# Seven half-width products for a pair of tiles: z, ga, gdn out and mix, and the attention's query and output

## The chip, the cores and the metric

One core of a Trainium2 chip runs the kernel. The metric is the device time of one execution in microseconds; the median of three runs stands for the kernel. A profile shows one execution, with every instruction of every engine. All data are float32.

## What is computed

Three blocks, one behind the other, on one sequence of 512 tokens and a width of 1024. The change lies in the first block: a gated feed-forward layer (ffn1), layer norm (ln1), "parallel mixers", layer norm (ln2), cross attention to a memory of 256 tokens, layer norm (ln3), a second feed-forward layer (ffn2), layer norm (ln4). Cut to what matters:

```python
def parallel_mixers(h, ...):
    proj = h @ w_in                       # qkv, z, a, bt, glu, gates
    ...
    o = chunk_gated_delta_rule(...)
    o = rms_norm(o, gdn_norm_g) * jax.nn.silu(z)
    y_a = o @ w_gdn_out
    ...
    y = jax.nn.sigmoid(g_a) * y_a + jax.nn.sigmoid(g_c) * y_c
    return y @ w_mix_out

def memory_cross_attention(x, mem, w_xq, w_xkv, w_xo):
    q = x @ w_xq
    k, v = jnp.split(mem @ w_xkv, 2, axis=-1)
    o = softmax(q @ k.T / 16) @ v         # 4 heads of 256
    return o @ w_xo
```

Both results y enter `x = layer_norm(2 ** 0.25 * x + y)`. The products in question are z, g_a (called ga), y_a (gdn out), the last line of the mixers (mix), q (xq) and the last line of the attention (xo): each a matrix of 1024 x 1024 on 512 tokens.

## The kernel before, in words

**Data.** Activations lie transposed: a tile has 128 features on the partitions and 512 tokens along them, so a vector of width 1024 is eight tiles. `X` (tiles 0 to 7) is the running activation; `main` is one large SBUF buffer in which `mem(at, tiles)` names places. Weights stream through four slots `w0` to `w3`, one load of 1 MB for each pair of output tiles (eight input tiles x two output tiles), issued by SyncE in the order in which TensorE takes the slots (`sp_weights`, L446): a load waits until the slot's last user is done ("w used"). PSUM has eight banks, handed out round robin (`banks.take`); whoever takes a bank waits for the "out" of its last user. Some stages confine the turn to a subset (`banks.only(range(2, 8))` in ssd and hgrn, `range(1, 8)` in rwkv), each subset with a counter of its own.

**Order.** Each engine has its program written out in order: `pe_...`, `act_...`, `dve_...` functions run over the same steps. Nothing is reordered; an engine that waits holds up all that stands behind it. Steps are named, and `wait_ge(*at(step))` waits for a named one.

**A pair** (`pe_pair`, the matmul at L262): for two output tiles f, eight matmuls each (k = 0 to 7) of 512 columns, 16 in all. Input tile k is waited for just before its matmul. ScalarE or VectorE then reads each bank.

**A step of seven** (`pe_seven`, the matmul at L338), used so far in the feed-forward layers and in the second and third blocks: input tiles are taken in pairs, tokens in two halves of 256, so that a pair of output tiles is a 2 x 2 block product, and the scheme of Strassen and Winograd gives it with seven products in place of eight. A product is four matmuls of 256 columns (one for each pair of input tiles), a step 28. The operands that are sums are made by VectorE: `dve_seven_weights` (L387, L388, L390, L392: four operations of 512 columns per step) and `dve_halves` (L401, L404, L406: once per pair of input tiles, not per step). The results are put together from four banks: `act_seven` copies the first one (L377), `dve_seven_out` does four operations (L422, L425, L427, L430), the last behind the last product. TensorE's order is product 1, 2 (from the input itself), 4 (needs all halves), 6 (needs the weight sums), 5, 7, 3. The sums have two places that alternate (`sets`).

**The mixers' end** (`pe_mixers`, L898). Behind the delta rule ("gdn", L1118 to L1298) come the head sums (L574), then the z pairs, with two spreads of the reciprocal root (L597) behind each, then ga, gdn out and mix, four pairs each. ScalarE takes z through SiLU (L998) and ga through a sigmoid (L1001). VectorE scales `O1` by the spread (L1060), multiplies it by the gate (L1064, "gated"), multiplies gdn out by its gate (L1068), adds the convolution's part (L1070, "mixed"), and at mix does the residual (`dve_residual`, L720) and a running total for the mean (L481). SyncE issues the loads of z only behind gdn (`input_here("after gdn")`).

**ln2 and ln3** (`pe_ln`): the sum of the total (L461) gives the mean, VectorE centres (L542), ScalarE squares (L499), TensorE adds the squares (L470), then root, reciprocal (L514), scaling (L547) and ScalarE's scale and bias (L535). At ln2 two pairs of xk run between mean and squares, and two behind the squares; they have 256 columns (the memory's tokens).

**The attention** (`pe_xattn`, L1357): xk's last two pairs, xq's four pairs with ScalarE's copies to `QT` (L1404), scores (L1372), softmax, values (L307), probabilities transposed (L1382), the attention's output (L1394), copied to `O2` by ScalarE (L1423), and xo's four pairs with VectorE's residuals (L720).

The lines that say how an engine takes a bank and how the residual is made:

```python
            for f in range(m):
                b, before = into[f]
                if kg == 0 and before:
                    pe.wait_ge(*at("out", *before))
                for k in range(kk):
                    pe.wait_ge(*at(*g.ready, kg + k))
                    i = pe.mm(PS[b][:, 0:n], wv[:, k, f * 128:(f + 1) * 128], g.X(kg + k),
                              start=kg + k == 0, stop=kg + k == g.nk - 1)
```

Of the kernel before, what the change touches and what calls it, by code (L numbers as in the profile page):

```python
# [14 lines left out]
TOK = 512  # L15
NT = 4
D = 1024
ALPHA = 2.0 ** 0.25
# [169 lines left out]
def assemble(nc, ctx, io, out):  # L188
# [27 lines left out]
    def mem(at_, tiles, width=TOK):  # L216
        return View(main[:, at_:at_ + tiles * width].rearrange("p (a b) -> p a b", b=width))

# [497 lines left out]
    def dve_residual(v, name, ready, total):  # L716
        for f in range(8):
# [132 lines left out]
    G_z = Gemm("z", w_in, 3072, 8, 8, X, x1)  # L850
    G_ga = Gemm("ga", w_in, 6160, 8, 8, X, x1)
    G_gout = Gemm("gdn out", io["w_gdn_out"], 0, 8, 8, O1, ("gated",))
    G_mix = Gemm("mix", io["w_mix_out"], 0, 8, 8, YC, ("mixed",))
# [44 lines left out]
    def pe_mixers(pe):  # L898
# [31 lines left out]
        for j in range(0, 8, 2):  # L930
            run(pe_pair(pe, G_z, j))
            for i in (j, j + 1):
                pe_head_spread(pe, "o1", i)
        run(pe_gemm(pe, G_ga))
        run(pe_gemm(pe, G_gout))
        run(pe_gemm(pe, G_mix))
        pe.fence("mix")

    def act_mixers(a):
# [56 lines left out]
        for f in range(8):  # L996
            a.wait_ge(*at("mm", "z", f))
            a.act(Z1(f), bank("z", f), ACT.Silu).then_inc(a.inc(s, "out", "z", f), 1)  # L998
        for f in range(8):
            a.wait_ge(*at("mm", "ga", f))  # L1000
            a.act(GA(f), bank("ga", f), ACT.Sigmoid).then_inc(a.inc(s, "out", "ga", f), 1)  # L1001
        a.fence("mix")

    def dve_mixers(v):
# [50 lines left out]
        s = sem["dve", "gdn"]  # L1055
        dve_head_root(v, "o1", 32, 7, 1.0 / 128, 1e-6)
        dve_head_rstd(v, "o1", 32)
        for h in range(8):
            v.wait_ge(*at("mm", "head", "o1", h))
            v.stt(O1(h), O1(h), par("gdn_norm_g"), bank("head", "o1", h), MUL, MUL).then_inc(  # L1060
                v.inc(s, "out", "head", "o1", h), 1)
            v.wait_ge(*at("out", "head", "o1", h))
            v.wait_ge(*at("out", "z", h))
            v.tt(O1(h), O1(h), Z1(h), MUL).then_inc(v.inc(s, "gated", h), 1)  # L1064
        for f in range(8):
            v.wait_ge(*at("out", "ga", f))
            v.wait_ge(*at("mm", "gdn out", f))
            v.tt(GA(f), GA(f), bank("gdn out", f), MUL).then_inc(v.inc(s, "out", "gdn out", f), 1)  # L1068
            v.wait_ge(*at("out", "gdn out", f))
# [2255 lines left out]
```

## Time and profile before

| what | us |
|---|---|
| median of three runs | 5203.94 (5198.2 to 5204.95) |
| the profiled execution, its own time | 5202.78 |
| its span in the trace | 5201.0 |
| TensorE busy (matmuls) | 4847.3, 93% of the span |
| VectorE busy | 2504.1, 48% |
| ScalarE busy | 880.7, 17% |
| DMA | 311.68 MB, mean 60 GB/s |

The span is the time between the first and the last instruction on the core. Matmuls are pipelined, so that the durations of single ones overlap; what tells their pace is the distance between starts. One matmul of the program leaves two records. In a timeline each row is a run of like instructions: start, time from the first start to the last end, engine, line, operation, operands with their shapes, number, and in brackets how long the engine stood idle before it and what released it.

### The profile page before, as it was taken

What the parts mean: (1) busy time and instruction counts of PE and PEld (TensorE: products, weight loads), DVE (VectorE), ACT (ScalarE), POOL (GpSimd) and SP (SyncE); (2) the same over time, 40 slices, a digit from 0 to 9 for tenths busy, and PEclk for the clock granted to TensorE, in tenths of its full rate; (3) what the DMA queues carried; (4) which work ended last, traced back from release to release, by engine and by line L of the source; (5) the groups of instructions that cost most, each with busy time, mean ns of one, the idle gap of its engine ahead of it and who ended that gap; (6) DMA issues with size and microseconds to landing.
All of it is one profiled execution on the core that took longest, in us unless ns stands there. A gap on an engine that the chain in (4) does not pass through costs nothing.

```text
span 5201.0 us, 57019 instructions
## 1 busy us (share of the span) xinstructions
PE 4847.3 (93%) x24452; PEld 3550.7 (68%) x24452; DVE 2504.1 (48%) x4208; ACT 880.7 (17%) x1533; POOL 146.6 (3%) x228
## 2 busy tenths in 40 slices
PE   8999999989999998999999999899997888888988
PEld 6885445774565885565555688688876877778743
DVE  5674874340204465562442556555554555555402
ACT  0001113120121002211221100010002323333210
POOL 0000000000000000000000000000000111111000
PEclk9998999989999998999999999998998999999999
DMA  6523541013222221112111222221220000000021
GB/s 229 174 93 53 69 62 41 1 24 74 95 76 73 89 83 55 57 33 65 42 42 49 77 85 89 73 81 65 89 73 29 1 1 1 1 1 1 17 92 41
DMA packets 284923, 311.68 MB, mean 60 GB/s; under 512 B 7168, under 2 KB 277632, under 8 KB 281472
## 3 DMA queue, kind: packets, MB, share of 16 engines
q1 hardware_dynamic: 284672, 308.04, 20.5%
q8 instruction: 193, 3.16, 0.2%
q14 instruction: 58, 0.48, 0.0%
HBM read 305.92 MB, written 2.10 MB: 59 GB/s over the span
## 4 chain that ended last, share of the span: by engine, by line
PE 51%; DVE 4%; ACT 3%; issue 0%; DMA 0%; SPq 0%; DVEq 0%; ACTq 0%
PE ps L338 18%; PE ps L262 12%; PE ps L753 4%; PE ps L766 2%; PE ps L740 1%; PE ps L1936 1%; PE ps L2732 1%; PE ps L307 1%; PE ps L461 1%; PE ps L2750 1%; PE ps L773 1%; PE ps L2971 1%; PE ps L1655 1%; PE ps L2477 1%; PE ps L1644 1%; PE ps L2663 1%
## 5 line engine op out<-in xcount | busy, mean ns | idle before, releaser
L262 PE MATMUL ps<-main,w 128*128 128x512 f32 (+1 forms) x3536 | 1547.0, 595 | 71.7 <-DMA w<-in_ffn_wg 18.8
L262 PEld LDWEIGHTS ps<-main,w 128*128 128x128 f32 x3536 | 675.2, 193 | 867.1 <-issue 836.8
L338 PE MATMUL ps<-main 128*128 128x256 f32 x4432 | 983.6, 379 | 0.0
L338 PEld LDWEIGHTS ps<-main 128*128 128x128 f32 x4432 | 841.7, 190 | 114.9
L338 PE MATMUL ps<-main,w 128*128 128x256 f32 x3344 | 745.7, 379 | 0.0
L338 PEld LDWEIGHTS ps<-main,w 128*128 128x128 f32 x3344 | 635.9, 190 | 89.2 <-issue 2.9
L425 DVE TENSOR_TENSOR main<-main,ps 128x512 f32<-128x512 f32 x142 | 97.7, 688 | 358.8 <-PE ps L338 358.6
L753 PE MATMUL ps<-main,w 128*128 128x128 f32 x1536 | 225.7, 295 | 4.4 <-DVE main L2836 2.2
L753 PEld LDWEIGHTS ps<-main,w 128*128 128x128 f32 x1536 | 203.6, 207 | 16.7 <-issue 5.8
L607 DVE SCALAR_TENSOR_TENSOR main<-main,params_sb 128x512 f32<-128x512 f32 x256 | 192.5, 752 | 9.1
L786 ACT COPY main<-ps 128x512 f32<-128x512 f32 x180 | 105.5, 586 | 520.9 <-PE ps L740 520.9
L766 PE MATMUL ps<-main 128*128 128x128 f32 x1440 | 190.2, 287 | 2.4 <-DVE main L812 2.4
L766 PEld LDWEIGHTS ps<-main 128*128 128x128 f32 x1440 | 178.5, 201 | 10.8 <-issue 7.5
L377 ACT COPY main<-ps 128x256 f32<-128x256 f32 x76 | 28.3, 372 | 729.1 <-PE ps L338 729.1
L740 PE MATMUL ps<-consts_sb,main 128*128 128x128 f32 x944 | 143.3, 279 | 7.0 <-DVE main L796 6.8
L812 DVE TENSOR_TENSOR main<-ps,consts_sb 128x256 f32<-128x256 f32 x200 | 83.5, 424 | 121.7 <-PE ps L753 121.2
L430 DVE TENSOR_TENSOR main<-main,ps 128x512 f32<-128x512 f32 x142 | 97.6, 687 | 66.7 <-PE ps L338 65.4
L422 DVE TENSOR_TENSOR main<-main,ps 128x512 f32<-128x512 f32 x76 | 52.2, 687 | 160.9 <-PE ps L338 158.1
L820 DVE TENSOR_TENSOR main<-main,ps 128x256 f32<-128x256 f32 x200 | 81.8, 420 | 80.3 <-PE ps L766 79.3
L740 PEld LDWEIGHTS ps<-consts_sb,main 128*128 128x128 f32 x944 | 113.9, 146 | 8.9 <-DVE main L796 7.6
L2903 DVE COPY_PREDICATED w<-consts_sb,ps 128x512 f32<-128x512 uint32 x128 | 85.7, 724 | 62.1 <-PE ps L2732 62.1
L377 ACT COPY tmp<-ps 128x256 f32<-128x256 f32 x66 | 24.6, 372 | 498.9 <-PE ps L338 498.9
(445 smaller groups left out, 5062.6 us busy)
## 6 DMA issues: line engine op xcount, KB each, us to landing
w<-in_w_in SPq DMA_DIRECT2D x58, 1024.0 KB, 6.4
w<-in_e_w_in SPq DMA_DIRECT2D x28, 1024.0 KB, 5.1
main<-in_ada_w SPq DMA_DIRECT2D x24, 1024.0 KB, 4.9
w<-in_ffn_wg SPq DMA_DIRECT2D x22, 1024.0 KB, 6.3
w<-in_ffn_wu SPq DMA_DIRECT2D x22, 1024.0 KB, 6.6
w<-in_o_w_in SPq DMA_DIRECT2D x20, 1024.0 KB, 5.4
w<-in_ffn_wd SPq DMA_DIRECT2D x16, 1024.0 KB, 5.2
w<-in_w_up SPq DMA_DIRECT2D x16, 1024.0 KB, 5.5
```

Of the source, the lines that this page charges most:

```text
L262: i = pe.mm(PS[b][:, 0:n], wv[:, k, f * 128:(f + 1) * 128], g.X(kg + k), start=kg + k == 0, stop=kg + k == g.nk - 1)
L338: t = pe.mm(PS[b][:, 256 * half:256 * half + 256], weight[:, m, :], x(m), start=m == 0, stop=m == n - 1)
L425: v.tt(inner, two(c[3]), b[2], ADD).then_inc(v.inc(s, "most", *step), 1)
L430: v.tt(inner, inner, b[3], ADD).then_inc(v.inc(s, "out", "seven", 3, *step), 1)
L607: v.stt(out, src[:, j:j + TOK], w(j), out, MUL, ADD).then_inc(v.inc(s, "tap", j, *step), 1)
L740: t = pe.tp(one(PS[b], i), one(src, i), ident)
L753: t = pe.mm(one(PS[b], i), one(MT, i), one(Dm, i), start=True, stop=True)
L766: t = pe.mm(one(PS[b], i), one(DT, i), one(x, i), start=True, stop=True)
L786: a.copy(DT[:, 0:n * 128], bank("inv t", m, *name)[:, 0:n * 128]).then_inc(a.inc(s, "out", "inv t", m, *name), 1)
L812: t = v.tt(own(x), own(b), mask.unsqueeze(1).broadcast_to([128, n, k, m]), MUL)
L820: v.tt(o, o, halves(b[:, 0:w], m, h), SUB).then_inc(v.inc(s, "out", "inv y", m, *name), 1)
L2903: v.pick(c3(MS[hd](kind)), mid(const(strict if kind < 2 else incl), 4).bitcast(U32), c3(bank("rw ms", i, k))).then_inc(v.inc(s, "out", "rw ...
```

## The change

Of the 24 pairs of z, ga, gdn out, mix, xq and xo, 22 become steps of seven; z's first and mix's first stay pairs. VectorE makes halves of X for z and ga (`BX`), of the gated `O1` for gdn out (`BO`), of the mixed `YC` for mix (`BX` again), of X behind ln2 for xq and of `O2` for xo (both `ATT`), and the weight sums of a step two steps ahead. What was done for one tile from a bank is now done for two tiles from SBUF: gate, product with the gate, sum, residual (`dve_seven_residual`). ScalarE copies the first product of each step; its copies of xq are gone.

```diff
@@ -215,6 +215,9 @@
         return View(main[:, at_:at_ + tiles * width].rearrange("p (a b) -> p a b", b=width))
+
+    def pairs_at(*at_):
+        return [[mem(o, 2)(i) for i in range(2)] for o in at_]
@@ -713,8 +716,24 @@
-    def dve_residual(v, name, ready, total):
-        for f in range(8):
+    def two_of(view, j):
+        return view.ap[:, j:j + 2, :]
+
+    def dve_seven_residual(v, g, j, room, ready, total):
+
+        v.wait_ge(*at(*room[1]))
+        dve_seven_out(v, g, j, 0, room[0])
+        v.wait_ge(*at("out", "seven", 3, g.name, j, 0))
+        for f in (j, j + 1):
+            v.wait_ge(*at(*ready, f))
+        v.stt(two_of(X, j), two_of(X, j), ALPHA, mem(room[0], 2).ap, MUL, ADD).then_inc(
+            v.inc(sem["dve", "dense"], "out", g.name, j), 1)
+        v.also("out", g.name, j + 1)
+        for f in (j, j + 1):
+            dve_total(v, total, f, X, ("out", g.name))
+
+    def dve_residual(v, name, ready, total, fs=range(8)):
+        for f in fs:
             v.wait_ge(*at(*ready, f))
@@ -847,10 +866,18 @@
     G_ab = Gemm("ab", w_in, 4096, 0, 8, X, x1, tok=True)
-    G_z = Gemm("z", w_in, 3072, 8, 8, X, x1)
-    G_ga = Gemm("ga", w_in, 6160, 8, 8, X, x1)
-    G_gout = Gemm("gdn out", io["w_gdn_out"], 0, 8, 8, O1, ("gated",))
-    G_mix = Gemm("mix", io["w_mix_out"], 0, 8, 8, YC, ("mixed",))
+    BS = [mem(12288 + 2048 * i, 4) for i in range(2)], [mem(36096 + 256 * i, 1, 256)(0) for i in range(2)]
+    BX, BO = pairs_at(*range(8192, 12288, 1024)), pairs_at(24576, 25600, 28800, 29824)
+    BF = mem(30848, 2).ap
+    G_z = Gemm("z", w_in, 3072, 8, 8, X, x1, seven=(*BS, BX, ("mixers x",)))
+    G_ga = Gemm("ga", w_in, 6160, 8, 8, X, x1, seven=(*BS, BX, ("mixers x",)))
+    G_gout = Gemm("gdn out", io["w_gdn_out"], 0, 8, 8, O1, ("gated",), seven=(*BS, BO, ("gdn y",)))
+    G_mix = Gemm("mix", io["w_mix_out"], 0, 8, 8, YC, ("mixed",), seven=(*BS, BX, ("mix y",)))
+
+    def mixer_steps():
+
+        return ([(G_z, j) for j in (2, 4, 6)] + [(g, j) for g in (G_ga, G_gout) for j in range(0, 8, 2)] +
+                [(G_mix, j) for j in (2, 4, 6)])
@@ -927,13 +954,14 @@
             pe_head_sums(pe, "o1", b, i, t512[i], ("o square", i))
-        for j in range(0, 8, 2):
-            run(pe_pair(pe, G_z, j))
-            for i in (j, j + 1):
-                pe_head_spread(pe, "o1", i)
-        run(pe_gemm(pe, G_ga))
-        run(pe_gemm(pe, G_gout))
-        run(pe_gemm(pe, G_mix))
+        run(pe_pair(pe, G_z, 0))
+        for g, j in mixer_steps():
+            if g is G_mix and j == 2:
+                run(pe_pair(pe, G_mix, 0))
+            run(pe_seven(pe, g, j))
+            if g is G_z:
+                for i in range(j - 2, j if j < 6 else 8):
+                    pe_head_spread(pe, "o1", i)
         pe.fence("mix")
@@ -993,12 +1021,15 @@
         act_head_root(a, "o1", 32)
-        for f in range(8):
+        for f in range(2):
             a.wait_ge(*at("mm", "z", f))
             a.act(Z1(f), bank("z", f), ACT.Silu).then_inc(a.inc(s, "out", "z", f), 1)
-        for f in range(8):
-            a.wait_ge(*at("mm", "ga", f))
-            a.act(GA(f), bank("ga", f), ACT.Sigmoid).then_inc(a.inc(s, "out", "ga", f), 1)
+        for g, j in mixer_steps():
+            act_seven(a, g, j)
+            if g in (G_z, G_ga):
+                gate, func = (two_of(Z1, j), ACT.Silu) if g is G_z else (two_of(GA, j), ACT.Sigmoid)
+                a.wait_ge(*at("out", "seven", 3, g.name, j, 0))
+                a.act(gate, gate, func).then_inc(a.inc(s, "out", g.name, j + 1), 1)
         a.fence("mix")
@@ -1053,22 +1084,58 @@
         s = sem["dve", "gdn"]
+        after(v, "gdn")
+        steps = mixer_steps()
+
+        def weights_of(n):
+            if n < len(steps):
+                dve_seven_weights(v, *steps[n])
+        for m in range(4):
+            dve_halves(v, ("mixers x",), X, BX, m, x1)
+        weights_of(0)
         dve_head_root(v, "o1", 32, 7, 1.0 / 128, 1e-6)
+        weights_of(1)
         dve_head_rstd(v, "o1", 32)
-        for h in range(8):
-            v.wait_ge(*at("mm", "head", "o1", h))
-            v.stt(O1(h), O1(h), par("gdn_norm_g"), bank("head", "o1", h), MUL, MUL).then_inc(
-                v.inc(s, "out", "head", "o1", h), 1)
-            v.wait_ge(*at("out", "head", "o1", h))
-            v.wait_ge(*at("out", "z", h))
-            v.tt(O1(h), O1(h), Z1(h), MUL).then_inc(v.inc(s, "gated", h), 1)
-        for f in range(8):
-            v.wait_ge(*at("out", "ga", f))
-            v.wait_ge(*at("mm", "gdn out", f))
-            v.tt(GA(f), GA(f), bank("gdn out", f), MUL).then_inc(v.inc(s, "out", "gdn out", f), 1)
-            v.wait_ge(*at("out", "gdn out", f))
-            v.tt(YC(f), YC(f), GA(f), ADD).then_inc(v.inc(s, "mixed", f), 1)
-        dve_residual(v, "mix", x1, "ln2")
+
+        def gated(j):
+            for h in (j, j + 1):
+                v.wait_ge(*at("out", "head", "o1", h))
+            v.wait_ge(*at("out", "z", j + 1))
+            v.tt(two_of(O1, j), two_of(O1, j), two_of(Z1, j), MUL).then_inc(v.inc(s, "gated", j), 1)
+            v.also("gated", j + 1)
+            dve_halves(v, ("gdn y",), O1, BO, j // 2, ("gated",))
+        used = None
+        for n, (g, j) in enumerate(steps):
+            if g is G_z:
+                dve_seven_out(v, g, j, 0, 16384 + TOK * j)
+                for h in range(j - 2, j if j < 6 else 8):
+                    v.wait_ge(*at("mm", "head", "o1", h))
+                    v.stt(O1(h), O1(h), par("gdn_norm_g"), bank("head", "o1", h), MUL, MUL).then_inc(
+                        v.inc(s, "out", "head", "o1", h), 1)
+                if j == 6:
+                    gated(0)
+            if g is G_ga:
+                dve_seven_out(v, g, j, 0, 20480 + TOK * j)
+                if j < 6:
+                    gated(j + 2)
+            if g is G_gout:
+                if used:
+                    v.wait_ge(*at(*used))
+                dve_seven_out(v, g, j, 0, 30848)
+                v.wait_ge(*at("out", "ga", j + 1))
+                v.wait_ge(*at("out", "seven", 3, g.name, j, 0))
+                v.tt(two_of(GA, j), two_of(GA, j), BF, MUL).then_inc(v.inc(s, "out", "gdn out", j), 1)
+                used = ("out", "gdn out", j)
+                v.wait_ge(*at(*used))
+                v.tt(two_of(YC, j), two_of(YC, j), two_of(GA, j), ADD).then_inc(v.inc(s, "mixed", j), 1)
+                v.also("mixed", j + 1)
+                dve_halves(v, ("mix y",), YC, BX, j // 2, ("mixed",))
+            if g is G_mix:
+                if j == 2:
+                    dve_residual(v, "mix", x1, "ln2", range(2))
+                dve_seven_residual(v, g, j, (30848, used), x1, "ln2")
+                used = ("out", "mix", j)
+            weights_of(n + 2)
         v.fence("mix")
@@ -1340,8 +1407,10 @@
     G_xv = Gemm("xv", io["w_xkv"], 1024, 0, 8, M, ("memory",), tok=True)
-    G_xq = Gemm("xq", io["w_xq"], 0, 8, 8, X, ("ln", "ln2"))
-    G_xo = Gemm("xo", io["w_xo"], 0, 8, 8, O2, ("out", "xo in"))
+    AS = [mem(o, 4) for o in (4096, 32896)], [mem(35968 + 256 * i, 1, 256)(0) for i in range(2)]
+    ATT = pairs_at(*range(28800, 32896, 1024))
+    G_xq = Gemm("xq", io["w_xq"], 0, 8, 8, X, ("ln", "ln2"), seven=(*AS, ATT, ("xattn x",)))
+    G_xo = Gemm("xo", io["w_xo"], 0, 8, 8, O2, ("out", "xo in"), seven=(*AS, ATT, ("xattn y",)))
@@ -1358,7 +1427,8 @@
             run(pe_pair(pe, G_xk, j))
-        run(pe_gemm(pe, G_xq))
+        for j in range(0, 8, 2):
+            run(pe_seven(pe, G_xq, j))
         for t in range(NT):
@@ -1393,15 +1463,15 @@
             m.then_inc(pe.inc(s, "mm", "xo in", f), 1)
-        run(pe_gemm(pe, G_xo))
+        for j in range(0, 8, 2):
+            run(pe_seven(pe, G_xo, j))
         pe.fence("xattn")
...
         act_xattn_keys(a, range(4, 8))
-        for f in range(8):
-            a.wait_ge(*at("mm", "xq", f))
-            a.copy(QT(f), bank("xq", f)).then_inc(a.inc(s, "out", "xq", f), 1)
+        for j in range(0, 8, 2):
+            act_seven(a, G_xq, j)
         for t in range(NT):
@@ -1421,11 +1491,25 @@
             a.copy(O2(f), bank("xo in", f)).then_inc(a.inc(s, "out", "xo in", f), 1)
+        for j in range(0, 8, 2):
+            act_seven(a, G_xo, j)
         a.fence("xattn")
...
         after(v, "mix")
+        steps = [(g, j) for g in (G_xq, G_xo) for j in range(0, 8, 2)]
+        dve_seven_weights(v, *steps[0])
+        for m in range(4):
+            dve_halves(v, ("xattn x",), X, ATT, m, ("ln", "ln2"))
+        dve_seven_weights(v, *steps[1])
+        for n in range(4):
+            g, j = steps[n]
+            dve_seven_out(v, g, j, 0, 10240 + TOK * j)
+            for f in (j, j + 1):
+                v.also("out", "xq", f)
+            if n < 2:
+                dve_seven_weights(v, *steps[n + 2])
         for t in range(NT):
@@ -1439,7 +1523,16 @@
             v.tt(ev, ev, bc(ssum, 256), MUL).then_inc(v.inc(s, "softmax", t), 1)
-        dve_residual(v, "xo", ("ln", "ln2"), "ln3")
+        for n in (4, 5):
+            dve_seven_weights(v, *steps[n])
+        for m in range(4):
+            dve_halves(v, ("xattn y",), O2, ATT, m, ("out", "xo in"))
+        used = ("halves", "xattn y", 3)
+        for n in range(4, 8):
+            dve_seven_residual(v, *steps[n], (34944, used), ("ln", "ln2"), "ln3")
+            used = ("out", "xo", steps[n][1])
+            if n < 6:
+                dve_seven_weights(v, *steps[n + 2])
         v.fence("xattn")
```

## Rows read from the trace of the kernel before

**Rows 1.** The page: busy time, share of the span and instructions of each engine.

```profile
PE 4847.3 (93%) x24452; PEld 3550.7 (68%) x24452; DVE 2504.1 (48%) x4208; ACT 880.7 (17%) x1533; POOL 146.6 (3%) x228
```

**Rows 2.** TensorE's timeline, 1130 to 1700 us: start, length, line, operation, count, idle before.

```profile
1167.49 15.88 PE L262 MATMUL ps<-main,w 128*128 128x512 f32 x32
...
1231.55 164.97 PE L262 MATMUL ps<-main,w 128*128 128x512 f32 x384
1398.12 1.10 PE L461 MATMUL ps<-tmp,consts_sb 128*128 128x512 f32 x2 [1.60 <-DVE tmp L481]
...
1412.86 7.03 PE L470 MATMUL ps<-tmp,consts_sb 128*128 128x512 f32 x16
1419.73 68.91 PE L262 MATMUL ps<-main,w 128*128 128x256 f32 x192
...
1533.41 13.90 PE L1394 MATMUL ps<-main 128*128 128x512 f32 x32
1547.14 55.10 PE L262 MATMUL ps<-main,w 128*128 128x512 f32 x128
1603.91 1.10 PE L461 MATMUL ps<-tmp,consts_sb 128*128 128x512 f32 x2 [1.67 <-DVE tmp L481]
1607.17 8.80 PE L470 MATMUL ps<-tmp,consts_sb 128*128 128x512 f32 x16 [2.17 <-ACT tmp L499]
...
1637.68 5.34 PE L338 MATMUL ps<-main,w 128*128 128x256 f32 x24
1642.87 7.07 PE L338 MATMUL ps<-main 128*128 128x256 f32 x32
1649.77 5.34 PE L338 MATMUL ps<-main,w 128*128 128x256 f32 x24
```

**Rows 3.** VectorE's timeline, 1395 to 1552 us, the end of mix and ln2.

```profile
1396.56 0.69 DVE L720 SCALAR_TENSOR_TENSOR main<-main,ps 128x512 f32<-128x512 f32 x1 [5.46 <-PE ps L262]
1397.28 0.69 DVE L481 TENSOR_TENSOR tmp<-tmp,main 128x512 f32<-128x512 f32 x1
...
1424.70 4.91 DVE L547 TENSOR_TENSOR main<-main,tmp 128x512 f32<-128x512 f32 x8
```

**Rows 4.** VectorE's timeline, 1600 to 1730 us, the start of ffn2.

```profile
1625.61 0.68 DVE L401 TENSOR_TENSOR main<-main 128x512 f32<-128x512 f32 x1
...
1627.13 0.68 DVE L401 TENSOR_TENSOR main<-main 128x512 f32<-128x512 f32 x1
...
1631.69 0.68 DVE L387 TENSOR_TENSOR main<-w 128x512 f32<-128x512 f32 x1
...
1634.35 0.68 DVE L387 TENSOR_TENSOR main<-w 128x512 f32<-128x512 f32 x1
...
1648.32 0.69 DVE L425 TENSOR_TENSOR main<-main,ps 128x512 f32<-128x512 f32 x1 [2.76 <-PE ps L338]
...
1649.97 0.69 DVE L430 TENSOR_TENSOR main<-main,ps 128x512 f32<-128x512 f32 x1 [0.51 <-PE ps L338]
1650.69 1.22 DVE L689 SCALAR_TENSOR_TENSOR main<-main 128x1024 f32<-128x1024 f32 x1
```

**Rows 5.** SyncE's loads at 1157 to 1158.5: the DMA view's issue, then its timeline row.

```profile
w<-in_w_in SPq DMA_DIRECT2D x1, 1024.0 KB, 19.8
...
1156.04 4.21 SPq L446 DMA_DIRECT2D w<-in_w_in  x1
```

**Rows 6.** TensorE's timeline, 2000 to 2100 us, the end of ffn2 and ln4.

```profile
2028.29 2.04 PE L461 MATMUL ps<-tmp,consts_sb 128*128 128x512 f32 x2 [3.67 <-DVE tmp L481]
2032.51 9.99 PE L470 MATMUL ps<-tmp,consts_sb 128*128 128x512 f32 x16 [2.17 <-ACT tmp L499]
```

**Rows 7.** ScalarE's timeline, 1395 to 1552 us: ln2's last operation, the last copy to O2.

```profile
1425.43 5.75 ACT L535 ACTIVATE main<-main,params_sb 128x512 f32<-128x512 f32 x8 [4.15 <-DVE main L547]
...
1547.34 0.58 ACT L1423 COPY main<-ps 128x512 f32<-128x512 f32 x1 [1.13 <-PE ps L1394]
```

**Rows 8.** Windows of 2 us: length, busy PE, PEld, DVE, ACT, POOL, granted clock, DMA, GB/s.

```profile
1170.00:1172.00 2.00, 2.00 (x4) 0.86 (x3) 0.00 (x0) 0.00 (x0) 0.00 (x0) 0.67 0.85 164
```

More of the change, by code:

```diff
@@ L2239, in assemble @@
     x3 = ("rms", "b2 final")
-    def pairs_at(*at_):
-        return [[mem(o, 2)(i) for i in range(2)] for o in at_]
     EX = pairs_at(*range(25608, 29704, 1024))
```

## The prediction

> **What bounds the kernel now.** I read the page's busy line first: TensorE is busy for 93% of the span, VectorE for 48% [rows 1]. Then TensorE's timeline through the two stages that the diff touches [rows 2]. There the twelve pairs of ga, gdn out and mix follow each other without a break: 384 records from 1231.55 us, 164.97 us long. A matmul of the program leaves two records, so a pair (16 matmuls of 512 columns) is 32 records, and it takes 164.97 / 12 = **13.74 us** (the last pipelined end included, a hundredth per pair). The four z pairs before them, the four pairs of xq (the second part of the row at 1419.73) and the four of xo (1547.14, 128 records in 55.10 us) go the same way. So TensorE alone sets the pace here, and what shortens a pair comes off the span in full. Only the ends of the two runs are not TensorE's: it stands idle for 1.60 and 1.67 us before the sum of the layer norm, for VectorE's residual and total [rows 2, 3].
>
> **What a step of seven costs.** The kernel already has the form, in ffn2. One step is 24 and then 32 records of 256 columns; the steps start at 1637.68 and 1649.77 [rows 2], **12.09 us** apart. Seven eighths of 13.74 is 12.02, so the narrower matmuls and 28 weight loads in place of 16 cost 0.07. A step saves 13.74 - 12.09 = 1.65 us.
>
> **The sum, part by part.**
> (1) 22 pairs change: three of z, four of ga, four of gdn out, three of mix (z 0 and mix 0 stay), four of xq, four of xo. 22 x 1.65 = **-36.3 us**. Nothing in rows 2 stands between these pairs to absorb it, and the weights (one 1 MB load per step, as before) are asked for four steps ahead.
>
> (2) VectorE's added work in a step: the four sums of weights have a period of 2.66 us (1631.69 to 1634.35); the four operations that gather the outputs are three like the 0.69 of L425 and one of 256 columns, below that, so under 2.8 [rows 4]. That is 5.4 us per step. Heaviest is gdn out, which adds two operations of 1024 columns (1.22 each, by L689) and three for the halves (a period of 1.52, 1625.61 to 1627.13): 5.4 + 2.5 + 1.5 = 9.4 us under TensorE's 12.09. The last z step adds four scalings (at most 1.22 each) and gated(0) with its halves, 2.7: 13.0 at the very most, once, and the ga step behind it has 5.4 + 2.7. So it costs nothing; if that cover were gone, each us over 12.09 would be one us per step.
>
> (3) The start of z: VectorE now makes halves of X (4 x 1.52 = 6.1 us), then sums of the second w_in load, then the root of the head sums, then sums of the third load, then the reciprocal. Those sums wait for loads issued right after gdn; the longest I see, issued at 1156.04, took 19.8 us and landed at 1175.8 [rows 5]. Behind it is the reciprocal, at about 1178.8. TensorE asked for it right behind z 0 (1183); now it asks behind the first step of seven, 1167.49 + 15.7 + 12.1 = 1195. **0 us**, with 16 us of room. ScalarE's root and SiLUs have the same room.
>
> (4) Between gdn out and mix: mix 0 needs the mixed tiles 6 and 7. Behind TensorE's last product VectorE does one gathering (0.69) and two operations of 1024 columns (1.22 each) [rows 4]: 3.2 us. Mix 0 takes k in order, and k = 6 is asked for after six matmuls of 0.86, 5.2 us. **0 us.** The halves of the mixed tiles (1.5 more) are only asked for behind all of mix 0.
>
> (5) The ends. Now VectorE does one residual and one total after the last product: TensorE ends at 1396.52, L720 starts at 1396.56, L481 at 1397.28, and the sum starts at 1398.12 [rows 2, 3]. After the change it does a gathering (0.72 start to start), a residual of 1024 columns (1.25), and two totals (0.72 and 0.69), with the same 0.2 around them: 3.57 us of idle in place of 1.60 and 1.67. Two ends: **+3.9 us**. The row at 2028.29, at the end of ffn2's steps of seven, shows 3.67 for a like chain [rows 6].
>
> (6) The start of xq: VectorE's scaling of ln2 ends at 1424.70 + 4.91 = 1429.6 [rows 3]; then the first weight sums (2.66), then halves of X, 4 x 1.52, to 1438.4. Its input is in time: ScalarE's last tile is done at 1431.2 [rows 7]. TensorE reaches xq at 1433.5 (xk's last two pairs, 64 records of 256 columns from 1419.73, take 13.8) and does two of the seven products before it needs the halves: 8 records of 0.216 each, twice, to 1437.0. **+1.4 us**; bounds 0 and 4.9 (if the first two products covered nothing).
>
> (7) The queries: gathered 0.7 us behind xq's last product, where ScalarE's copy of a tile takes 0.58 now [rows 7]. The scores that don't need tiles 6 and 7 cover 2.6 us (12 records of 0.216). **0.** The start of xo: its first product now waits for tile 6 of the input, its second for tile 7 (1547.9 [rows 7]), which is in time behind the first; VectorE's halves of tiles 6 and 7 end 1.6 us later, at 1549.6, and are asked for at 1547.14 + 3.5 = 1550.6. **0**, with 1.0 us of room.
>
> (8) TensorE's clock. The longer idle of (5) may let it fall from 2.4 to 1.2 GHz. The trace shows both outcomes: behind 1.60 us of idle it stayed; at ln3, behind 1.67 and 2.17, the squares took 8.80 us in place of the 7.03 of ln2; at ln4, behind 3.67, the sum took 2.04 in place of 1.10 and the squares 9.99 [rows 2, 6]. At ln2 matmuls of xk follow densely. What a fall costs there I take from the dense z 0, which ran into a low clock (granted 0.67 in the window to 1172 [rows 8]): 15.88 in place of the 13.90 of the 32 records at 1533.41 [rows 2], 2.0. Bounds 0 and 3.0 (9.99 against 7.03). I take **+2.0**: an idle of 3.6 us is nearer to ln4's. At ln3 the clock falls already; going from ln3's rows to ln4's adds (2032.51 - 2028.29) - (1607.17 - 1603.91) = 1.0 and 9.99 - 8.80 = 1.2. Bounds 0 and 2.2; I take the middle, **+1.1**, as the phase of the fall is open.
> The Trainium skill ("TensorE: Matmul & The Clock Gate", Why this matters for your kernels) speaks against this change here: it asks to leave no longer idle gaps between bursts of matmuls, as the clock goes back to its lower level. By that rule both ends would pay, which is the sum as taken; by the row at 1398.12 alone neither would, and the time would be 3.1 us less.
>
> Sum: -36.3 + 3.9 + 1.4 + 2.0 + 1.1 = **-27.9 us**. The profiled execution took 5202.78 (span 5201.0 and 1.8 around it), which is 1.2 under the median of the three runs, 5203.94. 5202.8 - 27.9 = 5174.9; I say **5175**.
>
> **Rivals.**
> *The clock stays up* and xq's start is covered: -36.3 + 3.9 = -32.4, 5170. For it: the trace holds at 1.60 us. Against: ln3 and ln4.
> *More is lost at the seams*: every bound of (6) and (8) at its dear end: -36.3 + 3.9 + 4.9 + 3.0 + 2.2 = -22.3, 5180; and the later stages, whose banks are now dealt out four places on (22 x 2 more takes of 8), wait up to a few us more in ssd, hgrn and rwkv, which use fixed subsets of banks: up to 5186.
> *Stalls inside the steps*: VectorE's in-order queue now also holds sums that wait for a load, and behind them the gatherings that free TensorE's banks. If each step stood for 1.2 us, the gain would be 22 x 0.45 - 8.4 = 1.5 us, 5201, no change. Against: ffn2 runs the same queue with no idle between steps, and loads land long before.
> *VectorE becomes the bound* (slower than before): a bank is free only once VectorE has gathered it, so TensorE would go at VectorE's pace. The point is 13.74 us of VectorE work per step; the dearest step has 9.4. If the operations ran 1.6 times as long beside these matmuls, the four gdn out steps would take 15.0, a loss of 1.3 each instead of a gain of 1.65; all steps would have to be like them to lose 22 x 1.3 + 8.4 = 37 us, 5240. Against: the durations in rows 4 were taken beside the same matmuls.
> *The change doesn't do what it says*: z 0 and mix 0 stay with eight products, which the sum has in it; the 22 others call the form that ffn2 uses. I see no other gap.
>
> **How the numbers follow.** Forecast (clock falls at one or both ends) 0.52; clock stays up 0.20; more lost at the seams 0.18; stalls inside the steps 0.05, nearly all of it within 0.2%; VectorE the bound 0.03; something I don't see 0.02. 0.2% is 10.4 us, about what a measurement of this kernel can tell from no change. The first three cases are all faster by more: 0.90, and a little of the fourth. Faster 0.91, same 0.06, slower 0.03. The range reaches from the second case, 5170, less 4 for the scatter of runs (5198.2 to 5204.95 before), to the end of the third: 5166 to 5186.
>
> **What would show it.** In the changed profile: steps of 56 records 12.1 us apart where pairs of 13.7 stood; no idle on TensorE between 1167 and the end of mix; an idle of 3.5 to 3.7 before both sums; about 1.4 us of idle between the second and third product of xq; the granted clock under 1 right behind ln2's sum; rows from ffn2 on as before, 26 to 29 us earlier. I am wrong if steps stand further apart than 12.2, if TensorE is idle for a weight sum or a bank, or if stages behind ffn2 change their length by more than 3 us.

## The result, and the profile after

| | before | after |
|---|---|---|
| median, us (executions) | 5204.44 (4) | 5158.11 (4) |
| lowest to highest | 5198.2 to 5205.78 | 5152.04 to 5167.63 |
| profiled execution; span | 5202.78; 5201.0 | 5155.09; 5152.9 |

The ratio is 0.9915, with an interval of 0.9899 to 0.9931: 46 us less, where 28 were forecast and the range, 5166 to 5186, took in 18 to 38. Faster was right, the size was not. (A second job, experiment 3 below, put it at 36.) One execution behind this document, 5344.6 us of the kernel before with the turn of the banks, at a mean granted clock of 0.921, fell into a slower state, and the ratios leave it out.

TensorE's timeline of the changed kernel, 1100 to 1650 us; the lines have moved: L265 is a pair's matmul, L341 a step of seven's, L464 the mean's sum, L473 the squares.

```profile
1167.34 15.87 PE L265 MATMUL ps<-main,w 128*128 128x512 f32 x32
1183.05 5.34 PE L341 MATMUL ps<-main,w 128*128 128x256 f32 x24
1188.23 7.07 PE L341 MATMUL ps<-main 128*128 128x256 f32 x32
...
1226.45 5.34 PE L341 MATMUL ps<-main,w 128*128 128x256 f32 x24
...
1238.54 5.34 PE L341 MATMUL ps<-main,w 128*128 128x256 f32 x24
...
1323.15 13.90 PE L265 MATMUL ps<-main,w 128*128 128x512 f32 x32
1336.88 5.34 PE L341 MATMUL ps<-main,w 128*128 128x256 f32 x24
...
1376.89 2.04 PE L464 MATMUL ps<-tmp,consts_sb 128*128 128x512 f32 x2 [3.58 <-DVE tmp L484]
1378.72 15.99 PE L265 MATMUL ps<-main,w 128*128 128x256 f32 x64
1394.55 7.03 PE L473 MATMUL ps<-tmp,consts_sb 128*128 128x512 f32 x16
1401.42 13.98 PE L265 MATMUL ps<-main,w 128*128 128x256 f32 x64
1415.23 3.62 PE L341 MATMUL ps<-main,w 128*128 128x256 f32 x16
1420.29 1.96 PE L341 MATMUL ps<-main,w 128*128 128x256 f32 x8 [1.44 <-DVE main L409]
...
1576.03 1.10 PE L464 MATMUL ps<-tmp,consts_sb 128*128 128x512 f32 x2 [3.59 <-DVE tmp L484]
1579.29 9.53 PE L473 MATMUL ps<-tmp,consts_sb 128*128 128x512 f32 x16 [2.17 <-ACT tmp L502]
1595.32 16.92 PE L265 MATMUL ps<-main,w 128*128 128x512 f32 x32 [6.50 <-ACT main L538]
1612.07 5.34 PE L341 MATMUL ps<-main,w 128*128 128x256 f32 x24
```

Set beside [rows 2], the changed stages do what was worked out. Steps stand 12.09 us apart (1226.45 to 1238.54) with no idle between them; mix 0 follows gdn out without a wait; the idle before the sums is 3.58 and 3.59; xq waits 1.44 for its halves (L409), after two products. And ln2's sum takes 2.04 us and xk's pairs 15.99, where they took 1.10 and 13.98. Two windows of 2 us around them give the granted clock (the third value from the end):

```profile
1376.00:1378.00 2.00, 1.11 (x2) 0.63 (x3) 0.71 (x2) 0.00 (x0) 0.00 (x0) 0.50 0.03 8
1378.00:1380.00 2.00, 2.00 (x5) 1.22 (x4) 0.40 (x1) 0.60 (x1) 0.00 (x0) 0.50 0.00 0
```

0.50 is the lower level, 1.2 GHz. ffn2's first step of seven starts at 1612.07 in place of 1637.68 [rows 2]: **25.6 us earlier**. The span is 48.1 shorter. So 22.5 us came from stages in which the program is the same, but for the numbers of the banks. Windows that cut both traces at the same matmuls show where; each is a stage, and its second value is its length. Before: ffn2's steps; ln4; the second block's ssd and hgrn; on to the rwkv rounds; rwkv; the end:

```profile
1637.70:2024.00 386.30, 386.30 (x1791) 340.08 (x1790) 205.74 (x325) 22.91 (x44) 0.00 (x0) 1.00 0.27 89
2024.00:2100.10 76.10, 51.81 (x100) 21.64 (x100) 37.32 (x58) 29.54 (x43) 0.00 (x0) 0.80 0.06 20
2100.10:2700.00 599.90, 569.78 (x3309) 348.47 (x3309) 267.92 (x418) 132.74 (x240) 10.00 (x32) 0.96 0.15 47
2700.00:4000.20 1300.20, 1226.38 (x5563) 975.48 (x5559) 673.94 (x1052) 125.82 (x225) 3.84 (x8) 0.96 0.23 73
4000.20:5007.10 1006.90, 883.32 (x7253) 763.59 (x7253) 510.38 (x1168) 304.17 (x516) 132.56 (x184) 0.95 0.03 9
5007.10:5201.00 193.90, 178.70 (x426) 81.22 (x426) 29.93 (x41) 21.93 (x42) 0.00 (x0) 0.96 0.17 58
```

After:

```profile
1612.10:1998.40 386.30, 386.30 (x1791) 340.07 (x1790) 205.76 (x325) 22.91 (x44) 0.00 (x0) 1.00 0.27 89
1998.40:2072.80 74.40, 50.11 (x101) 21.25 (x100) 37.31 (x58) 29.53 (x43) 0.00 (x0) 0.82 0.06 20
2072.80:2665.70 592.90, 562.92 (x3310) 343.37 (x3310) 267.91 (x418) 132.54 (x240) 10.00 (x32) 0.97 0.15 47
2665.70:3963.30 1297.60, 1223.88 (x5562) 973.82 (x5559) 673.96 (x1052) 125.81 (x225) 3.84 (x8) 0.96 0.23 73
3963.30:4958.80 995.50, 872.33 (x7252) 753.63 (x7252) 509.05 (x1168) 304.09 (x516) 132.54 (x184) 0.96 0.03 9
4958.80:5152.90 194.10, 178.88 (x426) 81.33 (x426) 29.93 (x41) 21.93 (x42) 0.00 (x0) 0.96 0.17 58
```

The changed kernel is 1.7 us shorter in ln4, 7.0 in ssd and hgrn, 2.6 up to rwkv and 11.4 in rwkv. VectorE's and ScalarE's busy times are the same to 1.4 us; TensorE's falls by what the stage falls, for the same matmuls. So they ran at a higher clock. Two theories: **clock** (the program comes to its later gaps at another time, and TensorE's clock falls at fewer of them) and **banks** (the 44 takes more deal the banks four places on, and waits for banks go away). The rival to both is **scatter**: there are four executions of each kernel, and one profile. The record of the executions supports it in part: those of the changed kernel ran at a mean granted clock of 0.964 (5152.0 and 5155.1 us), 0.962 (5161.1) and 0.961 (5167.6), so what sets executions of one kernel apart is the clock too, and the profiled one is among the short ones.

### The profile page after: what moved, and what is told of

The parts are those of the page before. It is cut to its first block, busy times and chain, and to the rows that moved or that the text cites. A ratio compares the mean times of both kernels' runs of the same rounds, so it can differ in the third digit from the quotient of the medians.

```text
span 5152.9 us, 58383 instructions
## 1 busy us (share of the span) xinstructions
PE 4794.3 (93%) x24980; PEld 3636.4 (71%) x24980; DVE 2641.4 (51%) x4425; ACT 882.8 (17%) x1540; POOL 146.6 (3%) x228
## 4 chain that ended last, share of the span: by engine, by line
PE 51%; DVE 4%; ACT 3%; issue 0%; DMA 0%; SPq 0%; DVEq 0%; ACTq 0%
PE ps L341 18%; PE ps L265 12%; PE ps L772 4%; PE ps L785 2%; PE ps L759 1%; PE ps L2822 1%; PE ps L2029 1%; PE ps L310 1%; PE ps L464 1%; PE ps L2840 1%; PE ps L792 1%; PE ps L1748 1%; PE ps L2567 1%; PE ps L1737 1%; PE ps L3061 1%; PE ps L2753 1%
## 5 line engine op out<-in xcount | busy, mean ns | idle before, releaser
L265 PE MATMUL ps<-main,w 128*128 128x512 f32 (+1 forms) x2832 | 1245.3, 596 | 70.8 <-DMA w<-in_ffn_wg 19.0
L341 PE MATMUL ps<-main 128*128 128x256 f32 x5136 | 1139.2, 379 | 0.0
L341 PEld LDWEIGHTS ps<-main 128*128 128x128 f32 x5136 | 975.5, 190 | 133.1
L265 PEld LDWEIGHTS ps<-main,w 128*128 128x128 f32 x2832 | 543.0, 195 | 700.0 <-issue 669.0
L341 PE MATMUL ps<-main,w 128*128 128x256 f32 x3872 | 862.7, 379 | 1.4 <-DVE main L409 1.4
L341 PEld LDWEIGHTS ps<-main,w 128*128 128x128 f32 x3872 | 735.2, 190 | 105.5 <-issue 4.3
L428 DVE TENSOR_TENSOR main<-main,ps 128x512 f32<-128x512 f32 x164 | 112.8, 688 | 417.0 <-PE ps L341 416.8
L772 PEld LDWEIGHTS ps<-main,w 128*128 128x128 f32 x1536 | 204.5, 208 | 16.4 <-issue 6.0
L425 DVE TENSOR_TENSOR main<-main,ps 128x512 f32<-128x512 f32 x98 | 67.3, 687 | 219.2 <-PE ps L341 216.4
L785 PEld LDWEIGHTS ps<-main 128*128 128x128 f32 x1440 | 170.3, 193 | 10.6 <-issue 7.5
L433 DVE TENSOR_TENSOR main<-main,ps 128x512 f32<-128x512 f32 x164 | 112.8, 688 | 78.8 <-PE ps L341 77.4
L390 DVE TENSOR_TENSOR main<-w 128x512 f32<-128x512 f32 (+1 forms) x164 | 111.2, 678 | 28.7 <-DMA w<-in_w_in 13.6
L839 DVE TENSOR_TENSOR main<-main,ps 128x256 f32<-128x256 f32 x200 | 81.3, 420 | 74.4 <-PE ps L785 73.4
```

The costliest lines, as they stand in the source:

```text
L341: t = pe.mm(PS[b][:, 256 * half:256 * half + 256], weight[:, m, :], x(m), start=m == 0, stop=m == n - 1)
L390: v.tt(S[0], a21, a22, ADD).then_inc(v.inc(s, "sum 0", *step), 1)
L428: v.tt(inner, two(c[3]), b[2], ADD).then_inc(v.inc(s, "most", *step), 1)
L433: v.tt(inner, inner, b[3], ADD).then_inc(v.inc(s, "out", "seven", 3, *step), 1)
L772: t = pe.mm(one(PS[b], i), one(MT, i), one(Dm, i), start=True, stop=True)
L785: t = pe.mm(one(PS[b], i), one(DT, i), one(x, i), start=True, stop=True)
```

## The experiments

Each kernel ran beside new executions of the kernel before. Its medians in four more jobs were 5197.0 (25 executions), 5196.7 (14), 5197.5 (11) and 5195.2 (9), so the 5204.4 of the first comparison lies 7 to 9 us above what it gave later.

**1. The turn of the banks, on either kernel.** At the end of the attention, ahead of its fence:

```diff
+        banks.i[tuple(range(8))] += 4
         pe.fence("xattn")
```

On the changed kernel this restores the old dealing from there on:

> The changed kernel, with the turn of the eight banks moved on by four places at the end of the attention, so that every bank behind it is dealt as in the kernel before. Nothing else changes. Clock theory (what was gained behind the attention, 22.5 us in the profiled execution, is TensorE's granted clock at other gaps because the program arrives earlier): the time stays where the changed kernel's is, 5152 to 5168, and the distance of the two traces still grows behind ffn2. Bank theory (the gain comes from banks dealt four places on, so that waits for banks fall away): the gain behind ffn2 is gone, 5155 + 22.5 = 5178.

On the kernel before it makes the new one:

> The kernel before with the same turn of four places. Clock theory: 5198 to 5206 as before. Bank theory: 5204 - 22.5 = 5182, without any step of seven added.

Measured: the changed kernel with the old dealing 5165.7 (4 executions, 5160.1 to 5175.6) against 5197.0, ratio 0.9938 (0.9921 to 0.9954); the kernel before with the new dealing 5197.9 (10 executions), ratio 1.0 (0.999 to 1.0009). Both times speak against the bank theory as it stood (5178 and 5182): the dealing alone gives nothing, and the changed kernel keeps most of its gain without it. But in the changed kernel ssd and hgrn (the second line) take 599.8 again, and rwkv (the fourth) stays short:

```profile
1996.30:2070.60 74.30, 50.01 (x100) 21.21 (x99) 37.26 (x58) 29.53 (x43) 0.00 (x0) 0.82 0.07 21
2070.60:2670.40 599.80, 569.57 (x3308) 348.42 (x3308) 267.70 (x418) 132.73 (x240) 10.07 (x32) 0.96 0.15 47
2670.40:3968.10 1297.70, 1223.86 (x5564) 973.81 (x5559) 674.01 (x1052) 125.82 (x225) 3.84 (x8) 0.96 0.23 73
3968.10:4963.50 995.40, 872.27 (x7253) 753.57 (x7253) 509.03 (x1168) 304.07 (x516) 132.57 (x184) 0.96 0.03 9
```

**2. The kernel before, later by a little dense work.** The first matmul of ga's first product is done two more times (four in the second kernel):

```diff
                     pe.wait_ge(*at(*g.ready, kg + k))
+                    if (g.name, j, f, k) == ("ga", 0, 0, 0):
+                        for _ in range(2):
+                            pe.mm(PS[b][:, 0:n], wv[:, 0, 0:128], g.X(0), start=True, stop=True)
```

> The kernel before with two matmuls of 512 columns repeated at the start of ga's first pair, 4 records or 1.7 us of dense work on TensorE, nothing else. Clock theory: all behind it arrives 1.7 us later with the same instructions, and the granted clock at the gaps behind falls out differently: the time moves by 1.7 plus something of either sign, up to 10 or 20 us, seen as low stretches of other lengths in ssd, hgrn and rwkv. Bank theory, and any theory in which the stages behind are indifferent to when they start: +1.7, 5206.

> The same with four matmuls repeated, 8 records or 3.4 us. Clock theory: +3.4 plus something of either sign, not twice what the run with two gave. Indifferent stages: +3.4, 5208.

Measured: 5202.2 (10 executions) and 5198.2 (10) against 5197.0, ratios 1.001 (1.0 to 1.002) and 1.0003. Neither time can tell a delay of 1.7 or 3.4 us from none. The traces are more telling: ssd and hgrn took 599.8 and 599.9, rwkv 1005.3 and 1012.7, and the stretch that was 2700 to 4000 before took 1297.7 and 1297.6, as in the kernel after. So 2.5 of the first comparison's 48.1 were that one execution. The delays did reach ssd, but not as they were. From z's start to ffn2's first step of seven the kernel before takes 470.2 us; with two matmuls more it took 473.4, which is 3.2 for the 1.7 added (ln3's squares took 10.17 for 8.80), and with four 473.6, the 3.4 added. The length of ssd and hgrn did not change with the time of arrival.

**3. The changed kernel again, and later.**

> The changed kernel once more, unchanged, to see it against the kernel before on one chip and over more executions (the first had four). Own-work theory: the change gives what its own stages show, 25 to 28 us, and what is more than that in the first four executions (46 by the medians) is mostly scatter of the stages behind: median difference 28 to 36. Rival: the 46 hold, because the stages behind are reached at another time and that is worth 15 to 20 us every time.

> The changed kernel with two matmuls of 512 columns repeated in mix's first pair: 1.7 us of dense work more. Own-work theory: 1.7 over the changed kernel, within its scatter of some 15 us. Rival (the time of arrival is worth 15 to 20 us by itself): the gain behind ffn2 moves by several us, either way, in all executions.

Measured: 5161.2 (6 executions, 5152.9 to 5175.1) against 5196.7, ratio 0.9930 (0.9914 to 0.9946), and 5162.1 (5153.3 to 5169.7). **The change is worth some 36 us here.** The executions of the changed kernel lie 16 to 22 us apart in a job, those of the kernel before 8 to 19; the first four of the kernel before lie high among its later ones. Whether that was chance or that job's chip was not told apart.

**4. The parts.** In one kernel only the mixers' 14 steps, in the other only the attention's 8; the other part is the kernel before's.

> Only the mixers' 14 steps of seven; the attention as before. By the terms of the prediction, at the start of ffn2 against the trace of before: 14 x 1.65 = 23.1 less, 2.0 more of idle before ln2's sum, 2.9 for the clock behind it: 18 us less. Whole time: 18 us less, and if the time of arrival counts by itself, another amount up to 15 us off that.

> Only the attention's 8 steps of seven; the mixers as before. At the start of ffn2: 8 x 1.65 = 13.2 less, 1.4 more of idle in xq, 1.9 before ln3's sum, 0 to 2.2 for the clock: 8 to 10 us less. Whole time: 8 to 10 less, and if the time of arrival counts by itself, another amount up to 15 us off that.

Measured: ffn2's steps start 17.5 us earlier (1620.2) and 9.3 earlier (1628.4), where 18 and 8 to 10 were expected; of these, 0.4 and 1.4 were there at z's start already, ahead of the edits. The times are 5177.9 and 5182.2 against 5196.7, ratios 0.9966 (0.9953 to 0.9979) and 0.9971 (0.996 to 0.9983): 19 and 15 us less. Together that is 33 us, near the 36 of the whole. The attention's part gives 5 to 7 us more than its own stages show; 2.1 of them stand in the profile at ln4, which took 74.0 in place of 76.1. The intervals are 6 to 7 us to either side, so the medians alone do not prove the rest.

**5. TensorE kept busy in the gaps.** In `pe_sum`, `pe_squares` and `pe_pair` of the changed kernel, matmuls of constants go into the bank that comes next; nobody reads what they make. One of the three edits:

```diff
+        for _ in range(4 if name in (("mean", "ln2"), ("mean", "ln3")) else 0):
+            pe.mm(PS[b], ones, consts[:, 0:TOK], start=True, stop=True)
```

> The changed kernel with matmuls on constants put where TensorE waits: four of 512 columns (3.4 us) before the mean's sum at ln2 and at ln3, two (1.7) before ln3's squares, seven (6.0) before ffn2's first pair. They compute nothing that is used. If the low clock behind these gaps is what the terms for the clock say, then against the changed kernel's trace: ln2's sum 1.10 in place of 2.04 and xk's pairs 13.98 in place of 15.99 (2.9 us less), ln3's squares 7 to 8 in place of 9.53, ffn2's first pair 13.9 in place of 16.92; ffn2's steps of seven start 6 to 8 us earlier. If the low clock has another cause, these rows stay. What the whole time does depends on the falls behind, 0 to 15 us less.

Measured in TensorE's timeline:

```profile
1373.03 3.60 PE L465 MATMUL ps<-consts_sb 128*128 128x512 f32 x8
1376.68 1.12 PE L468 MATMUL ps<-tmp,consts_sb 128*128 128x512 f32 x2
1377.64 13.98 PE L267 MATMUL ps<-main,w 128*128 128x256 f32 x64
...
1576.04 7.13 PE L479 MATMUL ps<-tmp,consts_sb 128*128 128x512 f32 x16 [0.36 <-ACT tmp L508]
1583.01 6.17 PE L264 MATMUL ps<-consts_sb 128*128 128x512 f32 x14
1589.58 14.00 PE L267 MATMUL ps<-main,w 128*128 128x512 f32 x32 [0.40 <-ACT main L544]
1603.42 5.34 PE L343 MATMUL ps<-main,w 128*128 128x256 f32 x24
```

xk's pairs take 13.98, the squares 7.13, ffn2's first pair 14.00: filling the gap takes the low clock away, so the gap was its cause, and the terms of (8) are prices of the clock. ffn2's steps start 8.7 us before the changed kernel's. **And the whole time is 5159.7 (6 executions), ratio 0.9924 (0.9911 to 0.9937), not clear of 5161.2.** In the profile ln4 took 76.0 again, ssd and hgrn 598.8 and the stretch up to rwkv 1299.0: that is 1.6, 5.9 and 1.4 more than in the changed kernel's, 8.9 together, so the 8.7 us were given back there. Rwkv took 1006.0, 10.5 more; the profiled execution is one of three near 5166, and the other three, 5153.8 to 5154.4, are no shorter than the shortest of the changed kernel (5152.0). The intervals by themselves would leave room for the 8.7 us; it is the trace that shows where they went.

**6. A pair of eight at the end instead.** Mix's and xo's last pairs are pairs again, with a residual and a total for each tile; at xq the halves come first.

```diff
-                [(G_mix, j) for j in (2, 4, 6)])
+                [(G_mix, j) for j in (2, 4)])
...
+        run(pe_pair(pe, G_mix, 6))
         pe.fence("mix")
...
+        dve_residual(v, "mix", x1, "ln2", range(6, 8))
         v.fence("mix")
...
-        dve_seven_weights(v, *steps[0])
         for m in range(4):
             dve_halves(v, ("xattn x",), X, ATT, m, ("ln", "ln2"))
-        dve_seven_weights(v, *steps[1])
+        for n in range(2):
+            dve_seven_weights(v, *steps[n])
```

> The changed kernel, with the last pair of mix and of xo as a pair of eight products again, so that one residual and one total follow TensorE's last matmul; and at xq the halves ahead of the weight sums. Against the changed kernel's trace at the start of ffn2: 2 x 1.65 dearer, 3.9 less of idle before the two sums, 2.9 less for the clock at ln2, 0.7 at ln3, 1.4 less of idle in xq: 5.6 us less. Banks behind the attention are dealt as in the kernel before (40 takes more, a multiple of 8): if that costs what the run with the turn showed in ssd and hgrn, 7 us come back.

> The same with the turn of the banks moved on by four at the end of the attention, so that they are dealt as in the changed kernel. Own-work theory: 5 to 6 us under the changed kernel's 5161. If the dealing matters only together with the time of arrival, this one and the one without differ by up to 7 us in ssd and hgrn in one direction or the other.

The idle before ln2's sum is 1.60 again and xk's pairs take 13.98, with no idle in xq (the run with the turn):

```profile
1374.60 1.10 PE L464 MATMUL ps<-tmp,consts_sb 128*128 128x512 f32 x2 [1.60 <-DVE tmp L484]
1375.53 13.98 PE L265 MATMUL ps<-main,w 128*128 128x256 f32 x64
1389.35 7.03 PE L473 MATMUL ps<-tmp,consts_sb 128*128 128x512 f32 x16
1396.21 13.98 PE L265 MATMUL ps<-main,w 128*128 128x256 f32 x64
1410.03 5.34 PE L341 MATMUL ps<-main,w 128*128 128x256 f32 x24
```

ffn2's steps start at 1603.7, 8.4 before the changed kernel's; 5.6 were expected. Two of the 8.4 were there at z's start already (1165.4 for 1167.3), so the edit gave 6.4. Without the turn: 5166.1 (5 executions), ratio 0.9933 (0.992 to 0.9945), no better than the changed kernel. With the turn: **5146.0 (4 executions, 5145.2 to 5148.4), ratio 0.9899 (0.9886 to 0.9912)**, better than both. The two do the same work and start ffn2 within 0.4 us of each other; ssd and hgrn took 599.8 without and 592.9 with the turn, rwkv 1009.1 and 995.4. The shortest executions, 5152.8 and 5145.2, are 7.6 apart, and 6.9 of that is ssd and hgrn.

**7. Both conditions in a third kernel.** Only the attention's steps, with the turn of experiment 1.

> Only the attention's 8 steps of seven, and the turn of the banks moved on by four at its end. The run without the turn has banks dealt as before, reached ln4 so that ln4 took 74.0 us where the kernel before takes 76.1, and gained nothing in ssd and hgrn. Theory of both together (the dealing saves 7 us there only if the program comes to ln4 in that way): ssd and hgrn 7 us less than in the run without the turn, 5182 - 7 = 5175. Theory that only the mixers' steps bring it: no gain there, 5182.

Measured: 5177.7 (5 executions) against 5195.2, ratio 0.9963 (0.995 to 0.9977), and against 5182.2 without the turn; 5175 was expected, and the intervals overlap. The trace is clear, ln4 and then ssd and hgrn, 7 us shorter than the 599.7 without the turn, as expected from both conditions together:

```profile
2018.30:2092.30 74.00, 49.71 (x100) 20.95 (x100) 37.33 (x58) 29.53 (x43) 0.00 (x0) 0.84 0.06 21
2092.30:2685.20 592.90, 562.90 (x3308) 343.40 (x3308) 267.79 (x418) 132.54 (x240) 10.07 (x32) 0.97 0.15 47
```

All fourteen profiles agree on the stage of ssd and hgrn:

| ln4 took | banks dealt as before | dealt four places on |
|---|---|---|
| 75.9 to 76.3 | 599.8, 599.9, 599.9 | 598.7, 598.7, 598.8 |
| 74.0 to 74.4 | 599.7, 599.8, 599.8 | 592.9, 592.9, 592.9, 592.9, 593.0 |

Where the new dealing acts first, ssd's first sums (L1721) wait for ScalarE's copy; TensorE's timeline of the changed kernel, and then of the same with the turn, in which that line is L1722:

```profile
2145.77 2.88 PE L1706 MATMUL ps<-consts_sb,main 128*128 128x128 f32 x12 [4.03 <-ACT main L1808]
2150.30 1.46 PE L1721 MATMUL ps<-main,consts_sb 128*128 128x16 f32 x6 [1.65 <-ACT main L1810]
```

```profile
2143.62 2.88 PE L1707 MATMUL ps<-consts_sb,main 128*128 128x128 f32 x12 [4.03 <-ACT main L1809]
2146.62 1.46 PE L1722 MATMUL ps<-main,consts_sb 128*128 128x16 f32 x6
```

The new dealing *adds* a wait of 1.65 us, and ends 7 us earlier 500 us on. The clock shows how. The window from 2600 to 2630 us covers the same gaps in the changed kernel and in the same with the turn; the rows of TensorE's timeline below each are the same matmuls:

```profile
2600.00:2630.00 30.00, 24.39 (x276) 15.87 (x276) 14.42 (x28) 7.10 (x14) 1.42 (x2) 1.00 0.11 37
2613.76 1.12 PE L2054 MATMUL ps<-main 128*64 128x64 f32 x16 [1.48 <-DVE main L2088]
2616.26 1.09 PE L2064 MATMUL ps<-consts_sb,main 128*128 128x128 f32 x8 [1.39 <-DVE main L2084]
```

```profile
2600.00:2630.00 30.00, 24.39 (x259) 17.02 (x258) 12.72 (x26) 7.17 (x13) 1.42 (x2) 0.83 0.11 36
2615.89 1.94 PE L2055 MATMUL ps<-main 128*64 128x64 f32 x16 [1.48 <-DVE main L2089]
2619.22 1.97 PE L2065 MATMUL ps<-consts_sb,main 128*128 128x128 f32 x8 [1.39 <-DVE main L2085]
```

The same gaps, 1.48 and 1.39 us, bring the lower clock in one kernel and not in the other. Added up from the traces' record of the clock, the lower level held for 34.1 us of ssd and hgrn in each of the five short profiles and for 51.2 in each of the nine others. Half of the 17.1 between them is 8.6 (at the lower level matmuls take about twice as long); less the wait of 1.65 that leaves 6.9, the difference that the windows show. So the cause of these 7 us is TensorE's clock, and the dealing of the banks matters by moving the gaps. That ln4 has to be left in the one way is seen in all fourteen profiles, but it was not changed by itself, and why it matters stays open.

## Why the prediction was wrong

**Terms (1) to (7) held.** A step takes 12.09 us, as taken. VectorE is not the bound: no step waits for it but xq's first. The start of z costs 0, though the third load's sums ran until 1180. Mix 0, the scores and xo cost 0. The two ends cost 3.90 for 3.9, and xq 1.44 for 1.4.

**Term (8), the clock, was undersized, by little.** ln2 cost 2.9 (0.94 in the sum, which I had left out, and 2.01 in xk) for 2.0. At ln3 the sum stayed at 1.10, the squares cost 0.7 more and ffn2's first pair, not in my sum, 1.5: 2.2 for 1.1. That this equals my upper bound is chance, as it is made of other rows. With 0.15 gained ahead of z, -36.3 + 3.9 + 1.4 + 2.9 + 2.2 - 0.15 = -26, against 25.6 measured and 27.9 forecast. By these stages the prediction was right.

**The step that failed** is the one that closed the sum and stands among its signs as "rows from ffn2 on as before". The stages behind had no term, and a rival gave the dealing of the banks only a loss of "up to a few us". I had written that the phase of a fall was open at ln3 and did not carry it to the many later gaps; my own sign of being wrong, stages behind ffn2 that change by more than 3 us, is there. In its place the runs show a clock that falls at fewer of these gaps: ln4 -1.7; ssd and hgrn -7.0, when the dealing and the way out of ln4 come together. -25.6 - 1.7 - 7.0 = -34.3, against 36 by the medians of the second job; as rwkv differs too from execution to execution, this agreement of one pair of profiles with medians is support and no proof. The first comparison's 46 has 10 us more; 7 to 9 of them are the kernel before's executions of that job, which is scatter and no part of the mechanism.

**The rule of the Trainium skill** ("TensorE: Matmul & The Clock Gate", Why this matters for your kernels), that longer idle gaps between bursts of matmuls bring back the lower clock, held where it was used: behind 3.58 and 3.59 us of idle both ends paid, and with the gaps filled they did not. It does not take a longer gap, though: in ssd and hgrn the clock was low behind gaps of 1.39 and 1.48 us. Experiment 5 limits the rule further: a gap that is kept warm is worth its price only if nothing behind it takes that back.

**Open.** rwkv took 995.4 to 995.7 us in six of the fourteen profiles and 999.0 to 1012.8 in the others. It goes with the clock: the lower level held for 73.8 to 74.1 us of it in the six and for 80.8 to 111.7 in the others. All profiles with short rwkv are of kernels with the mixers' steps, but two such kernels (experiments 5 and 6) had 1006.0 and 1009.1. The choice of the profiled execution is a rival to the change here: the six are executions within 3.3 us of the shortest of their kernel and job, and of the other eight seven are not. So the 11.4 us of the first pair of profiles can't be credited to the change. What makes one execution fall into the one or the other was not tried, and whether the last 2 us of the 36 are this is not settled.

## What to carry to other kernels

Price a change by its own stages, and then open the range by what the stages behind scatter by themselves: here 8 to 22 us between executions of one kernel in most jobs, and 7 us in one stage that no edit touched. Judge a saving of under a half per cent at the next fixed point of the trace (here the start of ffn2) and not by the total alone, and count it from a fixed point ahead of the edit (here z's start), as executions differ there already; 8.7 us gained at one point were gone by the start of rwkv. And where a cheaper form has a longer tail, the old form for the last tile can pay in its own stages: at ln2 it cost 1.65 us and saved 2.0 of idle and 2.9 of clock. In the total it paid only together with the turn of the banks.

## What the runs showed of the hardware

**Whether a gap brings the lower clock is not a matter of its length alone.** Behind gaps of 1.48 and 1.39 us the same matmuls took 1.12 and 1.09 us in one kernel, 1.94 and 1.97 in another; behind 3.67 us ln4's sum took 2.04 before and 1.10 after. So what stands ahead of a stage changes its length, for the same instructions.

**Earlier falls bring executions into step.** z started between 1164.7 and 1169.7 us in the fourteen profiles, but in all of them 10.0 to 10.1 us behind the last fall of the granted clock. From there the kernel before took 470.2 us to ffn2 in both of its profiles without a delay, though the starts were 2.3 us apart.

**A delay is not passed on as it is.** 3.4 us of added matmuls stayed 3.4 at ffn2 in the kernel before and 1.7 became 3.2; in the changed kernel 1.7 became 0.2, as ln2's sum took 1.27 for 2.04 and xk's pairs 15.53 for 15.99. Behind that, no stage from ln4 to rwkv changed by more than 0.2 us (74.2, 593.0, 1297.6, 995.7 against the 74.4, 592.9, 1297.6, 995.7 of the run beside it).

**Stages come in a few lengths,** not in a spread: 592.9, or 598.7 to 599.9, in ssd and hgrn. In rwkv it is 995.4 to 995.7 or something between 999 and 1013.
